# Gate and up products of a hybrid decoder layer on one Trainium2 core by Strassen's seven block products, with the hidden tiles kept in DRAM

## What is computed

```python
def swiglu(x, w_gate, w_up, w_down):
    return (jax.nn.silu(x @ w_gate) * (x @ w_up)) @ w_down

    x = x + 0.5 * swiglu(rmsnorm(x, ffn1_norm), ffn1_w_gate, ffn1_w_up, ffn1_w_down)
    u = rmsnorm(x, mix_norm)
    proj = u @ w_in
    ...
    x = x + jnp.concatenate([lru_out, ssd_out], axis=-1) @ w_out
    x = x + 0.5 * swiglu(rmsnorm(x, ffn2_norm), ffn2_w_gate, ffn2_w_up, ffn2_w_down)
```

## Time and profile before

| | |
|---|---|
| median of 3 runs | 2228.07 us (2228.02 to 2228.22) |
| span of the profiled execution | 2226.2 us, 1.9 us below the median |
| TensorE busy | 2211.9 us (99%), 14348 matmul records |
| VectorE, ScalarE, GpSimd busy | 1005.7, 524.5, 746.6 us |
| granted TensorE clock, mean | 0.998 |
| 100 to 200 us (FFN 1): VectorE, ScalarE, GpSimd busy | 34.19, 9.60, 31.01 us of 100 |

### The profile page before, as it was taken

One profiled execution on the slowest core, in us unless ns is written; L12 is line 12 of the kernel. 1 busy time (PEld: TensorE's weight loads), 2 busy tenths in 40 slices (PEclk: granted clock), 3 DMA queues, 4 the chain that ended last, 5 costly groups with the idle time before them and its releaser, 6 DMA issues.

```text
span 2226.2 us, 32201 instructions
## 1 busy us (share of the span) xinstructions
PE 2211.9 (99%) x14348; PEld 2178.7 (98%) x14348; DVE 1005.7 (45%) x786; ACT 524.5 (24%) x744; POOL 746.6 (34%) x418
## 2 busy tenths in 40 slices
PE   9999999999999999999999999999999999999998
PEld 8999999999999999999999999999999999999998
DVE  6522122321223557877888586862321132212336
ACT  4100001000001225678786440110000000000113
POOL 5333333332222323433435553223333333332240
PEclk9999999999999999999999999999999999999999
DMA  4111111111112332311112322111111111111122
GB/s 154 48 48 48 46 43 46 47 48 48 48 46 72 120 95 78 125 46 54 51 40 78 142 87 79 48 48 48 48 48 48 48 44 44 46 48 48 48 57 77
DMA packets 48602, 138.36 MB, mean 62 GB/s; under 512 B 7624, under 2 KB 16328, under 8 KB 48464
## 3 DMA queue, kind: packets, MB, share of 16 engines
q1 hardware_dynamic: 47312, 135.78, 19.3%
...
q10 hardware_dynamic: 1152, 0.52, 0.1%
...
## 4 chain that ended last, share of the span: by engine, by line
PE 91%; DVE 3%; ACT 2%; issue 1%; DVEq 1%; POOL 1%; POOLq 0%; ACTq 0%
PE set L605 85%; PE set L872 2%; ACT gate_a L1004 0%; PE pair L774 0%; ACT gate_x L1004 0%; DVEq L1428 0%; PE set L799 0%; DVE decay L1463 0%; POOL w_lo L501 0%; DVEq L1469 0%; DVE lru_conv L1310 0%; DVE x L1608 0%; DVEq L1309 0%; PE set L625 0%; DVE lru_even L1201 0%
## 5 line engine op out<-in xcount | busy, mean ns | idle before, releaser
L605 PE MATMUL set<-x_hi,w_lo 128*128 128x344 f32 x2064 | 659.3, 319 | 1.3 <-POOL w_lo L491 1.3
L605 PE MATMUL set<-x_hi,w_hi 128*128 128x344 f32 x2064 | 657.7, 319 | 0.0
L605 PE MATMUL set<-x_lo,w_hi 128*128 128x344 f32 x2064 | 657.4, 319 | 0.0
L489 POOL TENSOR_SCALAR w_hi<-w_raw 128x1024 fp32r<-128x1024 f32 (+1 forms) x173 | 187.0, 1081 | 1221.4 <-PE set L605 1185.7
L491 POOL TENSOR_TENSOR w_lo<-w_raw,w_hi 128x1024 fp32r<-128x1024 f32 (+1 forms) x180 | 433.5, 2408 | 173.6 <-DVE xbc L1434 123.3
L605 PEld LDWEIGHTS set<-x_hi,w_lo 128*128 128x128 f32 x2064 | 387.3, 188 | 1.9 <-issue 1.8
L605 PEld LDWEIGHTS set<-x_hi,w_hi 128*128 128x128 f32 x2064 | 387.3, 188 | 0.1
L605 PEld LDWEIGHTS set<-x_lo,w_hi 128*128 128x128 f32 x2064 | 387.3, 188 | 0.0
L605 PE MATMUL set<-h_hi,w_lo 128*128 128x344 f32 x948 | 302.7, 319 | 0.0
L605 PE MATMUL set<-h_hi,w_hi 128*128 128x344 f32 x948 | 302.1, 319 | 0.0
L605 PE MATMUL set<-h_lo,w_hi 128*128 128x344 f32 x948 | 301.9, 319 | 0.0
...
## 6 DMA issues: line engine op xcount, KB each, us to landing
...
x<-in_xt SPq DMA_DIRECT2D x8, 516.0 KB, 8.2
x_kept<-x SPq DMA_DIRECT2D x8, 516.0 KB, 4.9
mixed<-power SPq DMA_DIRECT2D x8, 516.0 KB, 3.0
```

Of the source, the lines that this page charges most:

```text
L489: pool.tensor_scalar(w_hi[s][:, 0:n], w_raw[s][:, 0:n], 1.0, 0.0, ALU.mult, ALU.add)
L605: end = pe.matmul(out[:, c, 0:CH], w[s][:, k * P:(k + 1) * P], x[:, kx, c * CH:(c + 1) * CH], start=(first and n == 0), stop=(last and n = ...
```

## The change

In each FFN the first two hidden tiles (j = 0, 1) are still computed by plain units, now in four chunks of 258 columns. The other 20 tiles go in 10 pairs of output tiles; for each pair the gate products, then the up products form a group q (20 groups). A group has a 2x2 block weight (two output tiles by two halves of the contraction, each 128x512) and a 2x2 block x (the two halves of the contraction by the two halves of the tokens, 516 columns each). Strassen's scheme (in Winograd's form) takes seven block products instead of eight: four sums of x blocks, made once per FFN (`mixes`), four sums of weight blocks per group (`weight_sums`, VectorE), and sums of products (`corners`, `last_corner`, VectorE, and two copies by ScalarE). GpSimd splits seven operands per group (`operand`) into a ring of six buffers; a product is 24 matmuls of 258 columns into one of four pairs of banks (`twos`).

All gate and up work of an FFN now comes before its down units. Hidden pairs are written to DRAM (`store_hidden`) and read back into two stage tiles (`load_hidden`), where high and low parts are taken, first by the places that x's operands leave. x itself is overwritten by working tiles and is read again from DRAM (`x_again`). In FFN 1 the squares are now added by GpSimd, with two square buffers instead of four.

```diff
+HT, QT = T // 2, T // 4
+NG = FT - 2
+RING = 6
...
+    d.hidden = nc.dram_tensor("hidden", [P, FT, T], F32, kind="Internal").ap()
...
+        banks = ctx.enter_context(nc.psum_tensor("banks", [P, 8, 512], F32))
+        set0, set1, pair = banks[:, 0:3, :], banks[:, 3:6, :], banks[:, 6:8, :]
         sets = (set0, set1)
+        twos = [banks[:, n:n + 2, 0:QT] for n in (0, 2, 4, 6)]
...
+            def store_hidden(f, i):
+                sp.wait_ge(*f.h_ready.past(i + 1))
+                for n in range(2):
+                    sp.dma_start(d.hidden[:, 2 * i + n, :], f.u[n][:]).then_inc(f.h_stored.sem, 16)
+
+            def load_hidden(f, j):
+                if j >= 2:
+                    sp.wait_ge(*f.hidden.past(j - 1))
+                sp.dma_start(f.stage[j % 2][:], d.hidden[:, j, :]).then_inc(f.stage_landed[j % 2].sem, 16)

...
+                for q in range(2, NG):
+                    group_weights(f, src, q)
+                    if q % 2 == 0:
+                        store_hidden(f, q // 2 - 1)
...
+            def down(f, src):
+                tag = f.tag
+                sp.wait_ge(*f.h_stored.past(32 * (NG // 2 - 1)))
+                for j in range(2):
+                    load_hidden(f, j)
+                store_hidden(f, NG // 2 - 1)
+                sp.wait_ge(*f.op_ready.past(NOPS))
+                for m in range(2):
+                    load(("d" + tag, 0, m))
+                for j in range(2, 8):
+                    load_hidden(f, j)
...
+                    sp.wait_ge(*f.done.past(NOPS))
+                    for m in (1, 5, 2, 6):
+                        x_again(f, src, m)
+                    store_hidden(f, NG // 2)
+                    for m in (0, 3):
+                        x_again(f, src, m)
+                    sp.wait_ge(*f.h_stored.past(32 * (NG // 2 + 1)))
+                    for m in (4, 7):
...
+            def operand(f, q, n):
+
+                o = 7 * q + n
+                first, second = f.raw[2 * q % 4], f.raw[2 * q % 4 + 1]
+                if o >= RING:
+                    pool.wait_ge(*f.done.past(o - RING + 1))
+                elif o >= 2:
+                    pool.wait_ge(used, U((("g" if o < 4 else "u") + f.tag, 1)) + 1)
+                if n in (0, 3):
+                    pool.wait_ge(*f.raw_landed[2 * q % 4].past(16 * (q // 2 + 1)))
+                if n == 6:
+                    pool.wait_ge(*f.raw_landed[2 * q % 4 + 1].past(16 * (q // 2 + 1)))
+                if n in (1, 2, 4, 5):
+                    pool.wait_ge(*f.sums_ready.past(q + 1))
+                src = (first[:, 0:512], second[:, 0:512], f.s[0][:], first[:, 512:1024], f.s[1][:], f.s[2][:],
+                       second[:, 512:1024])[n]
+                to = f.op[o % RING]
+                pool.tensor_scalar(to[:, 0, :], src, 1.0, 0.0, ALU.mult, ALU.add)
+                pool.drain()
+                pool.tensor_tensor(to[:, 1, :], src, to[:, 0, :].bitcast(F32), ALU.subtract).then_inc(f.op_ready.sem, 1)
...
+                if tag == "1":
+                    for k in range(1, KT):
+                        pool.wait_ge(squared["ffn1"], k + 1)
+                        if k >= 2:
+                            pool.wait_ge(added["ffn1"], k - 1)
+                        pool.tensor_tensor(f.tot[:], f.tot[:], f.c[k % 2][:], ALU.add).then_inc(added["ffn1"], 1)
...
+            def second_plain(f):
+                name = "ffn" + f.tag
+                pe.wait_ge(*f.taken.past(2))
+                plain(f, ("g" + f.tag, 1), f.g_at)
+                pe.wait_ge(*f.taken.past(4))
+                plain(f, ("u" + f.tag, 1), f.u_at, hook=lambda: norm_sum(f, name, KT - 1))
+
+            def group(f, q):
+                def product(n, tokens):
+                    o = 7 * q + n
+                    out = twos[o % 4]
+                    if o >= 4:
+                        before, m = divmod(o - 4, 7)
+                        if m < 2:
+                            pe.wait_ge(*f.copied.past(2 * before + m + 1))
+                        else:
+                            pe.wait_ge(*f.ev.past(5 * before + m - 1))
+                    pe.wait_ge(*f.op_ready.past(o + 1))
+                    w = f.op[o % RING]
+                    for k in range(4):
+                        hi, lo = tokens(k)
+                        for c in range(2):
+                            cols = slice(c * QT, (c + 1) * QT)
+                            for i, (part, x) in enumerate(((1, hi), (0, hi), (0, lo))):
+                                end = pe.matmul(out[:, c, :], w[:, part, k * P:(k + 1) * P], x[:, cols],
+                                                start=(k == 0 and i == 0), stop=(k == 3 and i == 2))
+                    end.then_inc(f.done.sem, 1)
+
+                def own(half, row):
+                    return lambda k: (f.bh[4 * half + k][:, row, :], f.bl[4 * half + k][:, row, :])
+
+                def mix(n):
+                    return lambda k: (f.th[k][:, n, :], f.tl[k][:, n, :])
+
+                if q == 0:
+                    pe.wait_ge(*f.rooted.past(2))
+                    if f.u_at[0] is twos[0]:
+                        pe.wait_ge(*f.taken.past(8))
+                product(0, own(0, 0))
+                if q == 0:
+                    pe.wait_ge(*f.taken.past(8))
+                    pe.wait_ge(*f.mix_lo.past(4))
+                product(1, mix(0))
+                product(2, mix(1))
+                product(3, own(1, 0))
+                product(4, mix(2))
+                product(5, own(1, 1))
+                product(6, mix(3))
...
+            def mix_high(f, k):
+                act.wait_ge(*f.mix_ready.past(k + 1))
+                act.activation(f.th[k][:], f.tf[k][:], ACT.Copy).then_inc(f.mix_hi.sem, 1)
...
             def first_square(k):
-                if k >= 5:
-                    act.wait_ge(added["ffn1"], k - 4)
-                act.activation(f1.ring[k % 4][:] if k else f1.tot[:], f1.x[:, k, :], ACT.Square).then_inc(squared["ffn1"], 1)
+                if k >= 3:
+                    act.wait_ge(added["ffn1"], k - 2)
+                act.activation(f1.c[k % 2][:] if k else f1.tot[:], f1.x[:, k, :], ACT.Square).then_inc(squared["ffn1"], 1)
...
+            def mixes(f, k, gain):
+
+                to = f.tf[k]
+                g0, g1 = (vecs[:, gain + n:gain + n + 1] for n in (k, k + 4))
+                dve.wait_ge(*f.t_first.past(k + 1))
+                dve.scalar_tensor_tensor(to[:, 0, :], f.x[:, k, 0:HT], g0, to[:, 2, :], ALU.mult, ALU.subtract)
+                dve.drain()
+                dve.scalar_tensor_tensor(to[:, 1, :], f.x[:, k + 4, HT:T], g1, to[:, 0, :], ALU.mult, ALU.add)
+                dve.scalar_tensor_tensor(to[:, 2, :], f.x[:, k + 4, HT:T], g1, to[:, 2, :], ALU.mult, ALU.subtract)
+                dve.drain()
+                dve.scalar_tensor_tensor(to[:, 3, :], f.x[:, k + 4, 0:HT], g1, to[:, 1, :], ALU.mult,
+                                         ALU.subtract).then_inc(f.mix_ready.sem, 1)
...
+            def weight_sums(f, q):
+
+                first, second = f.raw[2 * q % 4], f.raw[2 * q % 4 + 1]
+                a11, a12, a21, a22 = first[:, 0:512], first[:, 512:1024], second[:, 0:512], second[:, 512:1024]
+                for n in range(2):
+                    dve.wait_ge(*f.raw_landed[(2 * q + n) % 4].past(16 * (q // 2 + 1)))
+                if q:
+                    dve.wait_ge(*f.op_ready.past(7 * q - 1))
+                dve.tensor_tensor(f.s[1][:], a11, a21, ALU.subtract)
+                dve.drain()
+                dve.scalar_tensor_tensor(a21, a21, -1.0, a22, ALU.mult, ALU.subtract)
+                dve.drain()
+                dve.scalar_tensor_tensor(f.s[0][:], a21, -1.0, a11, ALU.mult, ALU.subtract)
+                dve.drain()
+                dve.tensor_tensor(f.s[2][:], a12, f.s[0][:], ALU.subtract).then_inc(f.sums_ready.sem, 1)
...
+            def hidden_pair(f, i):
+                dve.drain()
+                dve.wait_ge(*f.silu.past(i + 1))
+                for n in range(2):
+                    last = dve.tensor_tensor(f.u[n][:], f.g[n][:], f.u[n][:], ALU.mult)
+                last.then_inc(f.h_ready.sem, 1)
...
+            def corners(f, q, between=None):
+                dst = f.u if q % 2 else f.g
+                if q % 2:
+                    dve.wait_ge(*f.h_stored.past(32 * (q // 2 + 1)))
+                p1, p5, u2, u3 = f.p
+                out = [twos[(7 * q + n) % 4] for n in range(7)]
+                dve.wait_ge(*f.done.past(7 * q + 3))
+                dve.wait_ge(*f.copied.past(2 * q + 1))
+                dve.drain()
+                dve.tensor_tensor(halved(u2), out[2], halved(p1), ALU.add).then_inc(f.ev.sem, 1)
+                dve.wait_ge(*f.done.past(7 * q + 4))
+                dve.tensor_tensor(halved(dst[0][:, 0:HT]), out[3], halved(p1), ALU.add).then_inc(f.ev.sem, 1)
+                dve.wait_ge(*f.copied.past(2 * q + 2))
+                dve.drain()
```

(36 more changed lines are left out.)

540 lines of the change are left out of this document (373 added, 167 removed).

## The result

The changed kernel takes 2210.79 us (median, 2207.29 to 2215.96) against 2228.12: 17.3 us faster, a ratio of 0.9926 with a 95% interval of 0.9912 to 0.9940. Forecast were 2175.6, that is 52.5 less. The time lies in the range of 2140 to 2218 and on the side that was forecast, but two thirds of the gain are missing.

What follows compares the result with a forecast made beforehand. TensorE was taken as the bound, busy 99% of the span. Terms -96.9 + 21 + 1.9 + 5 + 13 + 3.5 = -52.5 took the median from 2228.07 to 2175.6 us, range 2140 to 2218.

Steps and rivals of the forecast that it cites:

- Columns, -96.9: Gate and up of both FFNs: 7488 matmuls at 0.1197 us replace 6336 at 0.1568, -96.9 us (-112.6 to -87.1).
- Both rivals on the step (0.1292 and 0.109): 258-column matmuls: step stays at 0.1292, 2247 us, chance 0.05; or falls to 0.109, 2096 us, chance 0.03.
- Start of FFN 1, +21: Up to FFN 1's second gate unit: sums on GpSimd and new mixes delay it, +21 us (12 to 24).
- Groups: Steady groups of both FFNs: nothing added, but little room, GpSimd needing 19.5 of 20.1 us.
- The port as bound: Groups: rival that VectorE instructions on the shared port cost GpSimd their whole duration, 22.0 us per group, 2251 us, chance 0.08.
- small waits in every group: Groups: rival that one microsecond is lost per group, 40 us in all, 2215.6 us, chance 0.14.
- Waits in groups 1 to 3, at the transitions and at FFN 2's start, 21.5: Both FFNs: +5 us in groups 1 to 3 of FFN 1, +13 from groups to down products, +3.5 at FFN 2's start.
- two waits: Each transition: 2 us lost at the first down units; third down unit gets its bank at 46.5 to 51, not 43.
- The clock, nothing: Whole kernel: the forecast's sum has no term for a lower TensorE clock behind waits.
- The middle part, "the same work": Between the FFNs: the middle part runs the same work, with no change in time.

Runs made afterwards that it cites:

- edit 4: Changed kernel with VectorE adding FFN 1's squares again, x's low parts ahead of the mixes, and ScalarE reading the first plain pair earlier: 2191.68 us.
- edit 7: Changed kernel with GpSimd repeating one of each group's seven subtractions: 2224.51 us.
- Experiments 1 and 2: 1: kernel before with four GpSimd-made waits per FFN, 2306.13 against 2226.51 us; 2: changed kernel with ten matmuls inside each third-down-unit wait, 2206.19 us.
- experiment 8: Changed kernel with an extra 128-column GpSimd copy in the middle part: ahead of its first products' splits 2209.45 us, ahead of the two z splits 2203.86 us.

## Why the prediction was right and wrong

- **Columns, -96.9: right.** The step at 258 columns is 0.1202, not 0.1197: 7488 x 0.0005 = 3.7 us less gain. Both rivals on the step (0.1292 and 0.109) are out. So is the gap by the formula of the Trainium skill (page "TensorE: Matmul & The Clock Gate", section "Back-to-back issue gap"), 110 ns for 258 columns; the section itself gives that formula for a single matmul and not for a stream of loads and matmuls, which the forecast left out.
- **Start of FFN 1, +21: right, in part by luck.** 17.7, by the mechanism named (the unit waits for ScalarE's read of the first gate, behind the high copies), and put back by edit 4. But the additions were put at 2.3 us each from 23.6 on, though their row has 2.47; they took 2.88 from 20.35 on and ended at 40.49 where the forecast has 39.7, two errors that cancel. The last mix came at 49.4, not 55.
- **Groups: right in the result, tight in the reason.** 20.2 us each, TensorE unbroken. GpSimd needs some 18.4 (86.2 of 100 us and 35 gaps of 0.14), not 19.5; edit 7 adds 1.4 per group without a wait within the groups. The port as bound and small waits in every group are out.
- **Waits in groups 1 to 3, at the transitions and at FFN 2's start, 21.5: the sizes failed.** They are 32.4: 5.7 in groups 1 to 3 (forecast 5), 3.3 at FFN 2's start (3.5), but 23.4 at the transitions to the down units (13), 11.6 in FFN 1 and 11.8 in FFN 2. There the forecast has two waits. The first came one product earlier than it said, at the last group's seventh product and not at the first down unit, and took 5.7 and 3.3 us: that product needs the third product's bank, which VectorE reads only behind four low parts of tiles read back.

```profile
490.62 2.90 DVE L1640 TENSOR_TENSOR h_lo<-stage,h_hi 128x1032 fp32r<-128x1032 f32 x1 [1.59 <-ACT h_hi L1212]
493.61 0.70 DVE L1609 TENSOR_TENSOR parts<-banks,parts 128x516 f32<-128x516 f32 x1
494.36 0.80 PE L850 MATMUL banks<-mix_hi,w 128*128 128x258 f32 x2 [5.74 <-DVE parts L1609]
```

  The second stands where it was forecast, at the third down unit, but the residual was later, 5.9 and 8.5 us. In FFN 2 the last hidden pair's way to DRAM and back leads there, in the chain of the changed kernel (start, length, what):

```profile
1951.73 9.99 DMA hidden<-up
1961.73 3.53 DMA stage<-hidden
1967.53 1.24 DVE x L1672
```

  SP sends for all eight tiles of x once more ahead of that store, which takes 10 us, not the 3.0 of the earlier trace rows; in FFN 1, behind four tiles, it takes 4.0. That the tiles make it slow is read from the order, not tested.
- **The clock, nothing: the step that failed.** The forecast priced a wait by its length. Eight stretches at 1.2 GHz follow waits from the second gate unit on. In seven of them, in the FFNs, the matmuls behind the first one (0.215 apart at 258 columns, 0.29 at 344) lose 14.7 us: 8.5 in FFN 1 and 6.2 in FFN 2. Experiments 1 and 2 show that this follows from TensorE's standstill. Before, the FFNs had no such wait behind the start, so no row of that trace held this price. Its one stretch at 1.2 GHz ahead of the end, at 832.7, came with no wait longer than 0.35 us in the 15 us ahead of it, but behind 64 matmuls of 8 columns (chain of the kernel before), so a standstill isn't the only thing that the low clock follows; this stretch was not studied further.

```profile
829.45 2.05 PE pair L709 x64
```

  The Trainium skill, page "TensorE: Matmul & The Clock Gate", section "HAM oscillation — how this bites in real kernels", tells of a kernel whose TensorE waits for a transfer at each step and starts each step at the low clock again; the traces here agree, and the forecast had read that page for the matmul's gap alone.
- **The middle part, "the same work": failed.** It is the same work, and took 6.4 us more, because one meeting on the port fell the other way (experiment 8). It may also be part of what spreads the runs; that isn't shown.

Sum of the miss: 10.9 for waits, 14.7 for the clock, 6.4 for the middle, 3.7 for the step, less 3.3 for the start, is 32.4 of 36.5. The other 4 us are about what is left: down units that step by 0.1574 rather than 0.1568 where the clock is 1.00 (some 2), the first step behind each of the eight waits in the FFNs (1.7) and the overlap lost at each (1.3). Why the down units step by more is open.
